# Three resident experts instead of two, with the first weight transfers moved into the mixer

## What is computed

```python
xn = rms_norm(x, norm1_g)
proj = xn @ w_in                      # 1024 x 7168: B, C, H, GLU_a, GLU_b, gates A and B
y_a = (B * causal_dwconv3(C * H)) @ w_out_a
v   = silu(layer_norm(causal_dwconv31(GLU_a * sigmoid(GLU_b)) + b))
y_b = v @ w_out_b + b_out_b
x   = x + (sigmoid(gA) * y_a + sigmoid(gB) * y_b) @ w_o
xn  = rms_norm(x, norm2_g)            # then 4 groups of 8 experts: best group, best 2 in it
for e in range(32):
    hdn = silu(xn @ w_gate[e]) * (xn @ w_up[e])            # 1024 x 512 each
    out = out + combine[:, e:e + 1] * (hdn @ w_down[e])    # 512 x 1024
y = rms_norm(x + out, final_norm_g)
```

## Time and profile before

| | us |
|---|---|
| median of 3 runs (lowest, highest) | 917.24 (916.07, 917.82) |
| the profiled execution, its own time | 915.21 |
| its span, from the first to the last recorded instruction | 913.5 |
| PE busy | 790.5 (87% of the span) |
| 16 DMA engines, mean rate over the span | 274 GB/s |
| granted TensorE clock, mean | 0.966 of full speed |

### The profile page before, as it was taken

How to read it: one execution, slowest core, us unless ns; L and a number is a source line. 1 busy time by engine, 2 the same in 40 slices (tenths; PEclk the granted TensorE clock), 3 DMA queues, 4 the chain that set the end, 5 groups by cost and what they waited for, 6 DMA issues and landing times.

```text
span 913.5 us, 21495 instructions
## 1 busy us (share of the span) xinstructions
PE 790.5 (87%) x8650; PEld 599.0 (66%) x8651; DVE 424.8 (47%) x1127; ACT 321.4 (35%) x556; POOL 258.2 (28%) x127
## 2 busy tenths in 40 slices
PE   4999999999999999799977676757799985998994
PEld 3999999999999998555544343434455543555552
DVE  3066897899942342425332322223243422344354
ACT  5332775464358333232221211111223221222323
POOL 3755899794867781000000000000000000000000
PEclk9999999999999999789998999999999999999997
DMA  8634243336333422928999999999988999999911
GB/s 249 208 127 138 94 138 125 108 102 202 118 95 137 138 76 62 425 112 366 424 421 422 421 422 422 422 422 422 422 331 320 425 422 422 422 422 422 400 51 69
DMA packets 53169, 249.94 MB, mean 274 GB/s; under 512 B 6599, under 2 KB 6599, under 8 KB 28561
## 3 DMA queue, kind: packets, MB, share of 16 engines
q1 hardware_dynamic: 49184, 244.86, 67.8%
q10 hardware_dynamic: 3953, 4.67, 1.7%
HBM read 246.76 MB, written 2.75 MB: 273 GB/s over the span
## 4 chain that ended last, share of the span: by engine, by line
PE 56%; DMA 28%; DVE 10%; ACT 3%; issue 2%; SPq 1%; POOL 0%; DVEq 0%
DMA ring<-in_exp_w_up 27%; PE bank L1232 23%; PE bank L1394 12%; DVE bank L928 7%; PE bank L1423 5%; PE bank L1348 4%; PE bank L1382 4%; PE bank L1230 4%; DMA raw<-in_w_in 1%; DVE ua L990 1%; PE bank L1299 1%; PE bank L1410 1%; PE bank L1355 1%; ACT w_hi L630 1%; PE bank L1293 1%
## 5 line engine op out<-in xcount | busy, mean ns | idle before, releaser
L1394 PE MATMUL bank<-ring,xe 128*32 128x256 f32 x2816 | 178.9, 405 | 81.5 <-DMA ring<-in_exp_w_up 72.5
L509 POOL TENSOR_TENSOR w_lo<-raw,w_hi 128x2048 fp32r<-128x2048 f32 x40 | 184.9, 4625 | 75.7 <-ACT w_hi L630 75.6
L1394 PEld LDWEIGHTS bank<-ring,xe 128*32 128x32 f32 x2816 | 101.7, 115 | 153.4 <-issue 112.0
L1232 PE MATMUL bank<-x_hi,w_hi 128*128 128x384 f32 x448 | 150.9, 337 | 1.5 <-POOL w_lo L509 1.3
L1232 PE MATMUL bank<-x_hi,w_lo 128*128 128x384 f32 x448 | 149.7, 334 | 0.0
L1232 PE MATMUL bank<-x_lo,w_hi 128*128 128x384 f32 x448 | 149.7, 334 | 0.0
L928 DVE SCALAR_TENSOR_TENSOR bank<-ub,vec,bank 128x256 f32<-128x256 f32 (+1 forms) x416 | 137.1, 413 | 0.0
L1141 DVE SCALAR_TENSOR_TENSOR hid<-bank,slot_coef,sig 64x256 f32<-64x256 f32 x44 | 21.5, 489 | 231.6 <-ACT sig L812 231.6
L630 ACT ACTIVATE w_hi<-raw 128x2048 fp32r<-128x2048 f32 x40 | 76.6, 1917 | 83.0 <-PE bank L1232 71.2
L1423 PE MATMUL bank<-ring,hidT 128*32 128x256 f32 x1408 | 94.2, 384 | 5.5
L1232 PEld LDWEIGHTS bank<-x_hi,w_hi 128*128 128x128 f32 x448 | 84.1, 188 | 2.9 <-POOL w_lo L509 1.5
(11 more groups left out here) (205 smaller groups left out, 975.3 us busy)
## 6 DMA issues: line engine op xcount, KB each, us to landing
ring<-in_exp_w_gate SPq DMA_DIRECT2D x64, 1024.0 KB, 20.0
ring<-in_exp_w_up SPq DMA_DIRECT2D x64, 1024.0 KB, 22.0
ring<-in_exp_w_down SPq DMA_DIRECT2D x64, 1024.0 KB, 24.1
raw<-in_w_in SPq DMA_DIRECT2D x28, 1024.0 KB, 5.1
raw<-in_w_out_a SPq DMA_DIRECT2D x4, 1024.0 KB, 5.1
raw<-in_w_out_b SPq DMA_DIRECT2D x4, 1024.0 KB, 5.0
raw<-in_w_o SPq DMA_DIRECT2D x4, 1024.0 KB, 5.0
out<-n_tok ACTq DMA_DIRECT2D x3, 512.0 KB, 2.7
```

Source lines behind the costliest of these rows:

```text
L509: pool.tensor_tensor(w_lo[u % NW][:, :, :], raw[u % NW][:, :, :], w_hi[u % NW][:, :, :].bitcast(F32), ALU.subtract).then_inc(lo_ready, 1)
L1232: ins = pe.matmul(b, wp[:, k % UK, cols], xp[:, k, :], start=start, stop=stop)
L1394: last = pe.matmul(GU[q * T:(q + 1) * T, :], xe[:, k, :], wide(slots[q // 2])[:, k, q % 2 * QE:(q % 2 + 1) * QE], start=(k == 0), stop=(k ...
```

## The change

Nine buffers of 2 MB hold the weights of three experts. Six still lie in the arena. `ring6` and `ring7` lie over `ua` and `ub`, the inputs of the two convolutions, and `ring8` over `x_tok` (the rows of x) and half of `stage`. What used to lie in `ua` and `ub` behind the convolutions moves: the scratch `sq` of the layer norm to the place of `in_hi`, and `gf`, `junk` and `rw` (final norm weights, scratch, router weights) to the place of `cvb`. `y_hi` and `y_lo` move to the other half of `stage`. `SETS` says which three buffers an expert uses. The 18 transfers for experts 0, 1 and 2 are written out one by one: four stand between the loads of units 32 to 35, behind waits for the convolutions and for the copies of their last rows, the others behind the loads of the units, each behind a wait for the last use of its piece of memory. The last two wait for the rows of x to have been taken into the sums (`combined`). SP then refills the buffers of the expert three back. PE's loop has 10 turns of three experts, reading four bounds in each, and experts 30 and 31 follow behind the loop.

The diff, cut to its core:

```diff
-    RING = 6
+    SETS = ((6, 7, 5), (4, 0, 2), (1, 3, 8))
+    RING = 9
+    IN_ARENA = 6
...
+        sq = at("sq", [P, KB, N], F32, arena_at + 3 * NW * UNIT + ACTS)
...
+        junk = at("junk", [P, D], F32, same_at + 2 * ACTS)
+        gf = at("gf", [P, D], F32, same_at + 2 * ACTS + 4 * D)
+        rw = at("rw", [P, KB, R], F32, same_at + 2 * ACTS + 8 * D)
+        x_tok_at = -(-nc.sbuf_base // 32) * 32
         x_tok = sb("x_tok", [P, NT, D])
+        stage_at = -(-nc.sbuf_base // 32) * 32
+        stage = sb("stage", [P, 2, D])
+        assert stage_at == x_tok_at + 4 * NT * D
+        y_hi = at("y_hi", [P, QE], F32R, stage_at + 4 * D)
+        y_lo = at("y_lo", [P, QE], F32R, stage_at + 4 * D + 4 * QE)
...
+        ring = [at(f"ring{i}", [P, 4096], F32, arena_at + 2 * UNIT * i) for i in range(IN_ARENA)]
+        ring += [at("ring6", [P, 4096], F32, ua_at), at("ring7", [P, 4096], F32, ua_at + 16384),
+                 at("ring8", [P, 4096], F32, x_tok_at)]
...
+            def first_weights(e, c, h):
+
+                slot = SETS[e][c]
+                sp.dma_start(ring[slot][:, h * 2048:(h + 1) * 2048], (w_dn if c == 2 else w_gu[c])[e, h])\
+                  .then_inc(weights_in[slot][h], 16)
+
+            TAPS_USED = {32: (0, 0), 33: (1, 0), 34: (0, 1), 35: (1, 1)}
+            X_LO_USED = CHUNKS.index(("gB", 1))
...
+                if u in TAPS_USED:
+                    sp.wait_ge(conv_b_ops, CONV_B_OPS)
+                    sp.wait_ge(product_added, PRODUCT_COUNT)
+                    sp.wait_ge(tails_ready, 2 + 4 * KB)
+                    first_weights(0, *TAPS_USED[u])
+
+            sp.wait_ge(grp_done, CHUNK_END[X_LO_USED])
+            first_weights(1, 0, 1)
+            sp.wait_ge(grp_done, CHUNK_END[NCH - 3])
+            first_weights(0, 2, 0)
+            first_weights(0, 2, 1)
+            sp.wait_ge(lo_ready, UNITS - 2)
+            first_weights(1, 1, 1)
+            sp.wait_ge(lo_ready, UNITS - 1)
+            first_weights(2, 0, 0)
+            sp.wait_ge(lo_ready, UNITS)
+            first_weights(1, 1, 0)
+            sp.wait_ge(grp_done, CHUNK_END[NCH - 2])
+            first_weights(1, 2, 0)
+            first_weights(2, 1, 1)
+            sp.wait_ge(half_done, NCH)
+            first_weights(1, 0, 0)
+            first_weights(1, 2, 1)
+            sp.wait_ge(grp_done, len(GROUPS))
+            first_weights(2, 0, 1)
+            first_weights(2, 1, 0)
+            sp.wait_ge(stage_out[0], 80)
+            sp.wait_ge(x_rows_ready, NT)
+            sp.wait_ge(ssq_ready, 2 * NT)
+            sp.wait_ge(combined, 1)
+            first_weights(2, 2, 0)
+            first_weights(2, 2, 1)
+
+            def expert_weights(e, side, last_item):
 
                 for c, h in ((0, 0), (1, 0), (0, 1), (1, 1), (2, 0), (2, 1)):
-                    slot = 3 * par + c
-                    if first:
-
-                        sp.wait_ge(lo_ready, UNITS)
-                        if slot:
-                            sp.wait_ge(grp_done, len(GROUPS))
-                    else:
-
-                        used = (down_half, down_done) if c == 2 else (gate_up_half, gate_up_done)
-                        sp.wait_ge(used[h], last_item)
+                    slot = SETS[side][c]
+
+                    used = (down_half, down_done) if c == 2 else (gate_up_half, gate_up_done)
+                    sp.wait_ge(used[h], last_item)
                     src = w_dn if c == 2 else w_gu[c]
-                    sp.dma_start(ring[slot][:, h * 2048:(h + 1) * 2048], src[e, h] if first else
+                    sp.dma_start(ring[slot][:, h * 2048:(h + 1) * 2048],
                                  src[bass.ds(e, 1), h, :, :].rearrange("e p x -> p (e x)"))\
                       .then_inc(weights_in[slot][h], 16)
 
-            expert_weights(0, 0, True)
-            expert_weights(1, 1, True)
             sp.wait_ge(tables_ready, 1)
-            with sp.Fori(1, NE // 2) as pair:
-                for par in range(2):
-                    last_item = sp.value_load(table[0:1, bass.ds(pair * 2 + (par - 1), 1)], min_val=1, max_val=MAX_ITEMS)
-                    expert_weights(pair * 2 + par, par, False)
+            with sp.Fori(1, NE // 3) as rnd:
+                for side in range(3):
+                    last_item = sp.value_load(table[0:1, bass.ds(rnd * 3 + (side - 2), 1)], min_val=1, max_val=MAX_ITEMS)
+                    expert_weights(rnd * 3 + side, side, last_item)
+            for e in range(NE // 3 * 3, NE):
+                last_item = sp.value_load(table[0:1, e - 2:e - 1], min_val=1, max_val=MAX_ITEMS)
+                expert_weights(e, e % 3, last_item)
...
-                    link(dve.reciprocal(sq[:, 2, :], sq[:, 0, :]))
+                    link(dve.reciprocal(sq[:, KB - 1, :], sq[:, 0, :]))
...
-            bounds = [pe.alloc_register(f"bound{c}") for c in range(3)]
-            with pe.Fori(0, NE // 2) as pair:
-                pe.reg_load(bounds, table[0:1, bass.ds(pair * 2, 3)])
-                first, middle, end = [pe.snap(x, min_val=0 if n == 0 else 1, max_val=MAX_ITEMS) for n, x in enumerate(bounds)]
-                for side, (a, b) in enumerate(((first, middle), (middle, end))):
-                    slots = [3 * side + c for c in range(3)]
-                    filled = pair * 16 + 16
-                    with pe.Fori(a, b) as i:
-                        item(i, slots, filled)
+            bounds = [pe.alloc_register(f"bound{c}") for c in range(4)]
+
+            def experts(e, n, filled):
+
+                pe.reg_load(bounds[0:n + 1], table[0:1, bass.ds(e, n + 1)])
+                at_item = [pe.snap(x, min_val=0 if c == 0 else 1, max_val=MAX_ITEMS) for c, x in enumerate(bounds[0:n + 1])]
+                for side in range(n):
+                    with pe.Fori(at_item[side], at_item[side + 1]) as i:
+                        item(i, SETS[side], filled)
+
+            with pe.Fori(0, NE // 3) as rnd:
+                experts(rnd * 3, 3, rnd * 16 + 16)
+            experts(NE // 3 * 3, NE % 3, NE // 3 * 16 + 16)
```

More of the change, by code:

```diff
@@ L153, in trunk_program @@
         arena_at = -(-nc.sbuf_base // 32) * 32
-        arena = sb("arena", [P, RING * 4096])
+        arena = sb("arena", [P, IN_ARENA * 4096])
         same_at = -(-nc.sbuf_base // 32) * 32
@@ L162, in trunk_program @@
         ACTS = 4 * KB * N
-        ring = [at(f"ring{i}", [P, 4096], F32, arena_at + 2 * UNIT * i) for i in range(RING)]
         raw = [at(f"raw{i}", [P, UK, HALF], F32, arena_at + UNIT * i) for i in range(NW)]
@@ L168, in trunk_program @@
         in_hi = at("in_hi", [P, KB, N], F32R, arena_at + 3 * NW * UNIT + ACTS)
-        assert 3 * NW * UNIT + 2 * ACTS <= RING * 2 * UNIT
+        sq = at("sq", [P, KB, N], F32, arena_at + 3 * NW * UNIT + ACTS)
+        assert 3 * NW * UNIT + 2 * ACTS <= IN_ARENA * 2 * UNIT
         x_hi = at("x_hi", [P, KB, N], F32R, same_at)
@@ L199, in trunk_program @@
         assert D // TILES == QE and KB // 2 == TILES
+        junk = at("junk", [P, D], F32, same_at + 2 * ACTS)
+        gf = at("gf", [P, D], F32, same_at + 2 * ACTS + 4 * D)
+        rw = at("rw", [P, KB, R], F32, same_at + 2 * ACTS + 8 * D)
+        x_tok_at = -(-nc.sbuf_base // 32) * 32
         x_tok = sb("x_tok", [P, NT, D])
+        stage_at = -(-nc.sbuf_base // 32) * 32
[3 more added lines that the diff above has]
+        y_lo = at("y_lo", [P, QE], F32R, stage_at + 4 * D + 4 * QE)
+        product = stage[:, :, :].rearrange("p a d -> p (a d)")[:, 0:NPS * N].rearrange("p (s n) -> p s n", s=NPS)
         first_new = n_tok[:, :, :].rearrange("p t d -> p (t d)")[:, 0:KB * STRIP_ROWS[0]].rearrange(
             "p (k n) -> p k n", k=KB)
+        ua_at = -(-nc.sbuf_base // 32) * 32
         ua = sb("ua", [P, KB * WA])
         ub = sb("ub", [P, KB * WB])
+        assert nc.sbuf_base >= ua_at + 2 * 16384
+        ring = [at(f"ring{i}", [P, 4096], F32, arena_at + 2 * UNIT * i) for i in range(IN_ARENA)]
+        ring += [at("ring6", [P, 4096], F32, ua_at), at("ring7", [P, 4096], F32, ua_at + 16384),
+                 at("ring8", [P, 4096], F32, x_tok_at)]
         tmp = sb("tmp", [P, HALF // P, N])
@@ L208, in trunk_program @@
         new_cols = [first_new, later_new[:, :, 0:STRIP_ROWS[1]], later_new[:, :, STRIP_ROWS[1]:]]
[L209 to L213, removed]
         vec = sb("vec", [P, KB, NV])
@@ L251, in both @@
             return t[:, 0:NP], t[:, NP:N].rearrange("p (s n) -> p s n", s=NS)
[L254 to L257, removed]
         spread_rows = x2T[:, 4:8, :]
@@ L452, in _ @@
                 sp.dma_start(raw[u % NW][:, :, :], w[:, k0:k0 + UK, c0:c0 + HALF]).then_inc(unit_in[u % NW], 16)
-            def expert_weights(e, par, first):
-                for c, h in ((0, 0), (1, 0), (0, 1), (1, 1), (2, 0), (2, 1)):
-                    slot = 3 * par + c
-                    if first:
-                        sp.wait_ge(lo_ready, UNITS)
-                        if slot:
-                            sp.wait_ge(grp_done, len(GROUPS))
```

(15 more changed lines are left out.)

## The result

The changed kernel takes 891.38 us (median of 4 runs, 890.72 to 893.07) against 916.65 (4 runs, 915.04 to 917.82) on the same chip. The ratio is 0.9727, 95% interval 0.971 to 0.9744. Forecast was 892.0, and for the span of the profiled execution 888.3; that span is 889.0.

What follows compares the result with a forecast made beforehand. The expert stage was taken as bound by weight transfers, the mixer by PE. One expert fewer to bring (14.92) and no gap (10.3) give 25.2 us: 917.24 - 25.2 = 892.0 us, range 887 to 900.

Steps and rivals of the forecast that it cites:

- The sum: End of the kernel: landing of expert 29 plus 78.0 us; span 913.5 - 25.2 = 888.3, median 892.0 us.
- the gaps: Weight stream, experts 17 to 23: 10.3 us of idle DMA engines with two sets, expected to vanish with three.
- Start of the stream: First refills stay at 407.07 and 425.10, PE's times, but bring experts 3 and 4; expert 4's up weights land at 437.3.
- Does it run dry: Expert stage: refills go out early enough that DMA engines never idle; smallest reserve 6.5 us, at the refill for expert 22.
- is PE in time: Experts 25 to 29: PE waits for weights a last time at expert 29, for about 2.9 us.
- rival A: Expert stage: gaps stay and only one expert's lead, 14.92 us, is gained; 902.3 us, chance 0.07.
- Landing of expert 29: Expert stream: 437.3 + 25 x 14.92 = 810.3 us, which is 25.2 us before 835.54.
- Loading in the mixer: Mixer: early transfers cost nothing and gain nothing; four between units 32 to 35 delay a unit load by at most 2.49 us.
- rival C: Mixer: the four moved transfers each hold up a unit, + 10 us; 902 us, chance 0.05.
- PE's loop: Expert stage: five fewer turns save 6.8 us of PE's time, nothing at the end; passage ahead of expert 30 stays 1.09 us.
- rival B: PE's longer loop body: jumps back or passages cost 1.3 us each, 5 behind expert 29's landing; 898.5 us, chance 0.11.
- Rivals D and E: D: stream rate falls, 922 us, chance 0.03. E: transfers were hidden, only PE's chain counts, 917 us, chance 0.02.

Runs made afterwards that it cites:

- delay_front: Changed kernel with clamped bounds and 8 extra 128x512 products on PE just ahead of the last seed, before the first item: 898.92 us.
- control: Changed kernel with one addition, PE clamping each bound it reads to at least zero: 892.2 us, ratio 0.9754 to the kernel before.
- control_again: The changed kernel with only PE's bounds clamped, run a second time, beside the kernel with moved seeds: 890.68 us, ratio 0.9722.
- late_start: Changed kernel with clamped bounds, three sets kept but none of their transfers loaded inside the mixer: 891.79 us, ratio 0.9743.
- two_one_item: Kernel before the change, with clamped bounds and every expert limited to one item, leaving out work: 869.87 us.
- two_sets_early: Changed kernel with clamped bounds, its new buffer places and early transfers, but only two sets: 915.67 us, ratio 1.0.
- delay_mid: Changed kernel with clamped bounds and 8 extra products on PE between the turns for experts 9 to 11 and 12 to 14: 892.58 us.

## Why the prediction was right

**The sum.** Its two terms, one expert of the stream (14.92) and the gaps (10.3), gave 25.2 us. Measured were 25.3 in the medians and 24.5 in the spans. The half of the argument that could be doubted was the second term, and the pair with one item per expert isolates the first. The mechanism was right. That the medians agree with the forecast to 0.1 us is luck: the landing of expert 29 gained 24.1 us, not 25.2, the passage behind it 0.4 that weren't forecast, and the runs of one kernel spread by 2 to 3 us.

**Start of the stream.** The refills at 407 and 425 stayed where they were. That they are PE's times, and that each us there goes into the end, is shown by delay_front, where they go out at 416.49 and 434.52 and the last item comes as much later as the first.

**Does it run dry, is PE in time.** No slice from 444 to 822 us is under 421 GB/s (slice 37, in which the stream slows to its end, has 410, where the prediction wanted 415 up to 840), and the last wait is at expert 29, 2.0 us where 2.9 were forecast. The reserve at expert 22 was smaller than the 6.5 us of the sum: its refill goes out at 690.41, not at 687.1, and the transfers ahead of it end at 697.16, not at 695.9. With the prediction's 2.3 us of start that leaves 4.4 us. It was enough, so rival A fell.

**Landing of expert 29.** Forecast 810.3, measured 811.46. The start of the sum was exact: the up weights of expert 4 have landed at 437.32, forecast 437.3. The term that was mis-sized is the stream behind them, 25 x 14.92 = 373.0 us, measured 374.1, and the difference arises in one step. The next transfer lands at 441.15, 3.83 us later and not 2.49. From there on the pace is the forecast one (14.91 us an expert). Ahead of the step a transfer's 16 landings lie 0.6 us apart, behind it 2.0, so a part of the transfers is late by some 1.3 us and stays so. In the trace a transfer of another queue falls into this stretch (the view of the queues, 437 to 440 us):

```profile
q1 hardware_dynamic: 168, 1.25, 99.7%
q8 instruction: 1, 0.02, 2.2%
```

It is one packet of 16 KB, at 437.94 us, and takes 1.07 us. The other traces with three sets have the same pair: such a packet at 437.82 and a step of 3.92 us in the control, at 438.72 and 3.90 in control_again, at 439.10 and 4.03 in late_start. With two sets no such packet falls between the second refill and the end of the stream; in the kernel before the landings of a transfer stay 0.3 to 0.7 us apart, and the check of the prediction (467.1) came out at 467.23. But two_one_item has one at 404.25, behind its first refill, and there the landings part from 0.75 to 1.50 us with a step of 3.28. So the step comes without the third set too. No run moves such a packet by itself; the cause is read from times that fall together. The price is paid once, since every transfer behind it is already queued, and about 1.3 us of the forecast 25.2 went there (14.91 in place of 14.92 gave 0.2 back). The Trainium skill, "DMA: Bandwidth & Descriptors", section "Queues, rings and completion order", says that a transfer runs on up to 16 engines that go through their own rings; these numbers agree with one engine that fell behind the others, though the records don't name the engine.

**Loading in the mixer.** Cost nothing, gain nothing: late_start (891.79) and two_sets_early (ratio 1.0) show both, and rival C fell. ACT copies unit 34 at 297.42 in the changed kernel, 297.67 before, and the first item starts at 393.81, 394.19 before.

**PE's loop.** Turns cost about the 1.16 + 0.2 that were taken: "issue" is 1.35 to 1.49 us in the chain (1.44 in the piece above). It is hidden, but for the passage ahead of expert 30, which costs 0.66 instead of 1.09. Repeats of an item cost nothing in the longer body either (9.01), so rival B fell. The rule of the Trainium skill, "Runtime: NRT & Kernel Launch", section "Instruction fetch mechanics", has its condition in a target outside the instructions held, and the trace suggests that the longer body is held whole: between 439 and 841 us, nine turns, there is no transfer of the instruction queue. In delay_mid, whose second loop is new code, four come at 565.63 to 599.44, within 40 us of its first item (561.68). That these packets are PE's code is inferred from such times; the trace doesn't say it. One more of them in the first pass, for the longer body, is the price that the prediction did not foresee. Waits were forecast at 55 us and are 53.9.

**Rivals D and E.** The rate is the same (14.91 us an expert), and the third set moves the end.

## What to carry to other kernels

When a stream of transfers is the bound, another buffer set is worth what it takes off the stream (one unit that is already there when the stream starts) plus the gaps that it closes; find both in the landings before building it. Loading earlier into idle time is worth nothing if the buffers would be full anyway by the time the first refills need the transfers. And idle time of an engine is no reserve as such: the same delay counts ahead of the first refill and behind the last landing, and not at all between them.

## What the runs showed of the hardware that was not expected

The granted TensorE clock in the 31 us of routing differs between executions of the same code: in control it is 0.79 from 382 to 386 us, in control_again 0.50. In the traces read here, the first item starts the later the lower this clock is (its product for the hidden rows at 400.1 to 402.6 us), and the stream carries that to the end of the kernel. Moving 2 us of PE's work into a pause went with 4.1 us less in the timed runs.

A packet of 16 KB in the instruction queue (1.07 us) that falls into a full stream of 1 MB transfers makes the next landing come 3.8 to 4.0 us behind the one before instead of 2.49, and this stays in every landing behind it as long as the stream is full. Where the landings of a transfer were 1.6 us apart already (delay_mid, 565.63), one more packet moved the next by 0.3 us. The same packet in a stretch in which the stream has slack leaves nothing: in the changed kernel one at 420.78 parts the landings to 1.90 us, and behind the next pause they are 0.51 apart.
